# Differential attention scores: one step per unit for both softmax maps, on the lower and the upper rows of the array

## The chip, the cores and the metric

The kernel runs on one core of one Trainium2 chip. The metric is the device time of one execution in microseconds (us); lower is better. The engines are called as in the profile: PE is the matrix engine, with PEld for its weight loads, DVE the vector engine, ACT the scalar (activation) engine, POOL GpSimd, SP the queue that issues the weight DMAs.

## The reference, cut to what matters

Two layers of a mixer run over 512 latent tokens and 128 context tokens. In each layer a normalised, modulated h goes into one wide projection and then four branches. The branch that is changed is differential attention with 4 heads, each with two softmax maps over the same values:

```python
s = jnp.einsum('bqhmd,bkhmd->bhmqk', qb, k) * scale      # m = 0, 1: two maps, d = 64 each
p = jax.nn.softmax(s, axis=-1)
a = p[:, :, 0] - lam * p[:, :, 1]
return jnp.einsum('bhqk,bkhe->bqhe', a.astype(v.dtype), v)
```

A latent query sees 640 keys, 512 latent ones and 128 cached context ones. A context query sees its own 128 keys. Each map has a maximum, an exponential and a sum of its own. Everything is float32.

## The kernel before, in words

The whole program is a list of steps that `plan()` writes; every engine walks the same list in the same order and issues what it has to do in each step, so the order on each engine is fixed and an engine that waits holds all that is behind it. `SIGNALS` says how far each step moves each semaphore.

The work is tiled by 128 tokens. Tokens are tiles t = 0 to 3 (latent) and t = 4 (context). Differential attention runs over units u = 0 to 19, head f = u // 5 and tile t = u % 5. The two maps of a head lie on partitions 0 to 63 and 64 to 127 of `QT` (queries, transposed) and of `KTt` and `cK` (latent and cached keys). `differential()` writes for each unit:

- S of map 0, a place for filler work, TP of unit u-1, S of map 1, a place for filler work, PV of unit u-1. After that, for heads after the first, one part of the normalisation of the head before (NR, parts 0, 1 and 2 behind tiles 0, 1, 2) or, behind tile 4, the transposition of that head's result (YT).

The steps do the following.

- S (PE lines 1608 to 1649): 640 scores into PSUM banks 4 and 5 as one row (`scores`), as a product of 512 columns (L1647) and one of 128 (L1648); for t = 4 one of 128 (L1645). PE first waits until every exponential issued so far is done, since it overwrites the same banks. DVE takes the negated maximum (L1249), ACT takes the exponential with that bias and its sum (L952) into `Pm`. For map 1, DVE then waits for the exponentials, makes the reciprocals (L1254) and a factor (L1258) and folds map 1 into map 0 (L1261), which raises `comb`.
- TP: PE transposes the combined 128 x 640 in five pieces into banks 6 and 7 (L1666); ACT copies them to `AT` (L965).
- PV: PE multiplies by the values, five products of 128 (L1675), into a part of bank 7; DVE scales the result out (L1271) and raises `pvfree`.

The filler work is the projections of this and the next branch: `interleave()` spreads 64 parts of 12 PE instructions each (F: gate features; M: merge gates; P: output projections) over the 43 places. Their results sit in two double banks (0 and 1, 2 and 3). ACT takes a tanh of F and M (L911, L976), DVE combines F and P (L1203, L1411). They need weights: SP loads 512 KB pieces into `raw` (two buffers), ACT rounds one to `whi` (L771), POOL makes the remainder `wlo` (L701), four pieces ahead.

In layer 0 the same stage also holds 18 steps DM: each is two products with a sum on DVE (L1032) over one piece of the modulation weights, which comes through `raw` like the others. `layer_middle()` puts one behind every S step until they run out.

```python
for n, step in enumerate(rest):
    s.append(step)
    if step[0] == "S" and n < before:
        s += some(1)
```

The neighbourhood branch, later in the layer, has scores of two heads issued in turn on the two halves of the rows into banks 4 and 5 (L1638, L1641). The change leaves it as it is.

## Time and profile before

| | |
|---|---|
| median of 3 runs | 2116.16 us (2113.1 to 2120.86) |
| the profiled execution | 2114.92 us, of which 2113.1 us from the first to the last instruction |
| PE busy | 1972.8 us (93%) |
| DVE, ACT, POOL busy | 948.2, 640.1, 606.4 us |
| mean granted clock of PE | 0.976 |
| differential attention, layer 0 | about 264 to 492 us |
| differential attention, layer 1 | about 1299 to 1492 us |

How to read it: PE is busy nearly all the time and almost all of the chain that ended last runs through it. The share over the whole program says nothing on a single stage, though. In the first half of the stage in layer 0, PE is much less busy than elsewhere and DVE more.

### The profile page before, as it was taken

How to read it: one execution, taken by the hardware profiler on the slowest of the kernel's cores; microseconds unless marked ns; L12 is line 12 of the kernel's file. 1: busy time of each engine (PE TensorE's matmuls, PEld its weight loads, DVE VectorE, ACT ScalarE, POOL GpSimd, SP SyncE). 2: the span in 40 equal slices, each digit the busy share in tenths (PEclk: the TensorE clock that was granted, in tenths of full speed). 3: DMA queues.
4: the chain of work that ended last, by engine and by line, in shares of the span. 5: the costliest groups of instructions: out<-in, count | busy, mean ns of one | idle time of the engine just before them, and what ended most of it. 6: DMA issues, size and time to landing. Idle time of an engine off the chain costs nothing.

```text
span 2113.1 us, 30534 instructions
## 1 busy us (share of the span) xinstructions
PE 1972.8 (93%) x12364; PEld 1782.6 (84%) x12364; DVE 948.2 (45%) x1489; ACT 640.1 (30%) x1085; POOL 606.4 (29%) x286
## 2 busy tenths in 40 slices
PE   2798988999999999999978999999999999999998
PEld 0597777889888999899967977888898899989996
DVE  3866478454444564330242233455344555433122
ACT  3421232333343321221343222333243332213121
POOL 2632311223222233233323232222222223313331
PEclk7899999999999999999998999999999999999999
DMA  7234333112121122122322221111222112211231
GB/s 276 80 110 145 102 128 120 51 40 91 64 67 51 61 99 70 44 67 75 125 90 90 75 81 67 37 48 41 80 71 71 51 61 89 71 51 60 80 102 78
DMA packets 50956, 172.13 MB, mean 81 GB/s; under 512 B 6656, under 2 KB 7296, under 8 KB 50816
## 3 DMA queue, kind: packets, MB, share of 16 engines
q1 hardware_dynamic: 40736, 145.55, 20.6%
q10 hardware_dynamic: 10080, 24.63, 3.3%
q8 instruction: 98, 1.61, 0.3%
q14 instruction: 42, 0.34, 0.1%
HBM read 162.82 MB, written 7.34 MB: 81 GB/s over the span
## 4 chain that ended last, share of the span: by engine, by line
PE 77%; DVE 14%; issue 3%; DMA 2%; ACT 2%; POOL 1%; ACTq 0%; DVEq 0%; SPq 0%; POOLq 0%
PE ps L1573 53%; PE ps L1461 4%; PE ps L1463 3%; PE ps L1462 3%; DVE mixed L1032 3%; PE ps L1647 2%; PE ps L1666 2%; DMA raw<-in_wstream 2%; PE ps L1675 1%; PE ps L1685 1%; DVE Pm L1291 1%; DVE qr L1196 1%; DVE nmax L1249 1%; PE ps L1727 1%; DVE rt L1187 1%
## 5 line engine op out<-in xcount | busy, mean ns | idle before, releaser
L701 POOL TENSOR_TENSOR wlo<-raw,whi 128x1024 fp32r<-128x1024 f32 x224 | 560.6, 2503 | 1324.4 <-ACT whi L771 1322.4
L1573 PE MATMUL ps<-bufB,whi 128*128 128x320 f32 x2816 | 540.0, 314 | 7.0 <-DVE vn L1144 4.0
L1573 PE MATMUL ps<-bufA,whi 128*128 128x320 f32 x2816 | 540.9, 314 | 2.6 <-DVE z L1411 1.4
L1573 PEld LDWEIGHTS ps<-bufB,whi 128*128 128x128 f32 x2816 | 441.7, 189 | 16.9 <-issue 11.9
L1573 PEld LDWEIGHTS ps<-bufA,whi 128*128 128x128 f32 x2816 | 442.4, 189 | 12.7 <-issue 7.8
L1573 PE MATMUL ps<-bufB,wlo 128*128 128x320 f32 x1408 | 322.7, 310 | 0.0
L1573 PE MATMUL ps<-bufA,wlo 128*128 128x320 f32 x1408 | 322.6, 310 | 0.0
L771 ACT ACTIVATE whi<-raw 128x1024 fp32r<-128x1024 f32 x224 | 237.4, 1060 | 267.2 <-PE ps L1573 120.1
L1573 PEld LDWEIGHTS ps<-bufA,wlo 128*128 128x128 f32 x1408 | 237.3, 189 | 0.0
L1573 PEld LDWEIGHTS ps<-bufB,wlo 128*128 128x128 f32 x1408 | 237.1, 189 | 0.0
L952 ACT ACTIVATE Pm<-ps,nmax 128x640 f32<-128x640 f32 (+2 forms) x160 | 100.0, 625 | 367.2 <-DVE nmax L1249 329.4
L1411 DVE SCALAR_TENSOR_TENSOR z<-gate_m,ps 128x640 f32<-128x640 f32 x48 | 39.4, 821 | 230.0 <-PE ps L1573 229.9
L1249 DVE TENSOR_REDUCE nmax<-ps 128x1 f32<-128x640 f32 (+2 forms) x160 | 97.8, 611 | 93.4 <-PE ps L1648 65.5
L1461 PE MATMUL ps<-whi,bufA 128*128 128x512 f32 x240 | 99.4, 414 | 16.4 <-POOL bufA L736 8.4
L1032 DVE CUSTOM_DVE_ANT_0 mixed<-raw,mixed 128x1024 f32<-128x1024 f32 x64 | 94.7, 1479 | 32.5 <-DMA raw<-in_wstream 30.7
L976 ACT ACTIVATE gate_m<-ps 128x640 f32<-128x640 f32 x64 | 45.1, 705 | 192.8 <-PE ps L1573 189.7
L1461 PE MATMUL ps<-whi,bufB 128*128 128x512 f32 x240 | 95.7, 399 | 4.4 <-DVE rt L1187 3.8
L1463 PE MATMUL ps<-whi,bufA 128*128 128x512 f32 x240 | 97.3, 405 | 0.0
L1462 PE MATMUL ps<-wlo,bufA 128*128 128x512 f32 x240 | 97.0, 404 | 0.0
L1463 PE MATMUL ps<-whi,bufB 128*128 128x512 f32 x240 | 94.0, 392 | 0.0
L1462 PE MATMUL ps<-wlo,bufB 128*128 128x512 f32 x240 | 94.0, 392 | 0.0
L1647 PE MATMUL ps<-KTt,QT 64*128 64x512 f32 x128 | 72.7, 648 | 13.1 <-ACT Pm L952 11.2
(206 smaller groups left out, 1954.1 us busy)
## 6 DMA issues: line engine op xcount, KB each, us to landing
raw<-in_wstream SPq DMA_DIRECT2D x256, 512.0 KB, 3.3
stage<-in_w_mod SPq DMA_DIRECT2D x16, 512.0 KB, 15.4
out_y_sample<-X ACTq DMA_DIRECT2D x8, 512.0 KB, 2.7
Pm<-in_rpb ACTq DMA_DIRECT2D x12, 256.0 KB, 2.8
X<-in_x_sample SPq DMA_DIRECT2D x4, 512.0 KB, 12.5
xres<-in_x_sample ACTq DMA_DIRECT2D x4, 512.0 KB, 5.3
xres<-out_y_sample ACTq DMA_DIRECT2D x4, 512.0 KB, 5.5
tabs<-in_dft ACTq DMA_DIRECT2D x2, 965.5 KB, 4.6
```

Of the source, the lines that this page charges most:

```text
L701: pool.tensor_tensor(wlo[:, s % SPLITS, :], raw[:, PLAN.entry["W", s] % RAWS, :], whi[:, s % SPLITS, :].bitcast(F32), ALU.subtract).then_i ...
L771: act_e.activation(whi[:, s % SPLITS, :], raw[:, e % RAWS, :], ACT.Copy).then_inc(sems["hi"], 1)
L952: act_e.activation(dst, src, ACT.Exp, bias=nmax[:, slot:slot + 1], accum_out=esum[:, slot:slot + 1]).then_inc(sems["expd"], 1)
L976: act_e.activation(halves(gate_m[:, m % 2, :]), dsplit(b), ACT.Tanh, scale=0.5).then_inc(sems[f"free{b}"], 1)
L1032: yield dve.tensor_tensor_reduce(dots_out, src, rows[:, c, :], 0.5, 0.0, ALU.mult, ALU.add, mods[:, l, 2 * m + c:2 * m + c + 1])
L1249: dve.tensor_reduce(nmax[:, slot:slot + 1], src, AX_X, ALU.max, negate=True).then_inc(sems["nmax"], 1)
L1461: pe.matmul(out, stat_hi, mov_hi, start=first, stop=False)
L1462: pe.matmul(out, stat_hi, mov_lo, start=False, stop=False)
L1463: return pe.matmul(out, stat_lo, mov_hi, start=False, stop=last)
L1573: ins = pe.matmul(ps[:, 2 * b + n, 0:HALF], wt[:, cols], src[:, part, base + k, n * HALF:(n + 1) * HALF], start=k == 0 and wt is hi and pa ...
L1647: pe.matmul(scores[:, 0:DEC], q, KTt[row:row + 64, f, 0:DEC], start=True, stop=True)
L1666: ins = pe.transpose(dst[:, c * P:(c + 1) * P], src[:, c * P:(c + 1) * P], ident[:])
```

## The change

S becomes one step for both maps.

- PE issues the latent keys in two pieces of 256, each piece for map 0 (partitions 0 to 63, bank 4) and then map 1 (64 to 127, bank 5), and signals `sready`. Then it waits for `atready` and `pvfree`, issues the 128 context scores of both maps into the ends of banks 6 and 7 (`ctx_scores`), and signals again.
- DVE takes one maximum over the two banks (128 x 2 x 512), one over the context scores that ACT has copied to `Pm`, and the smaller of the two negated ones. Only after that ACT starts its exponentials: two of 512, and two of 128 over the copied scores, each pair with its own signal and its own sums. DVE waits for all four, adds the sums, and goes on as before.
- ACT has a new copy of the context scores (128 x 2 x 128), and the copy of the transposed weights is cut in two, since those lie in two banks now (384 and 256 columns). TP also waits for `copied`.
- In the plan, a unit is now: S, place, TP of u-1, place, PV of u-1. The number of places and the fillers in them are the same: two parts between S and TP, one between TP and PV in nearly every unit. DM now stands behind S and behind PV.

The diff, cut to its core (allocations, the list of semaphores and lines that only move are left out):

```diff
-    ("S", "diff", False, 0): {"expd": 1, "nmax": 1, "sready": 1},
-    ("S", "diff", False, 1): {"chain": 1, "comb": 1, "expd": 1, "nmax": 1, "sready": 1, "stat": 1},
+    ("S", "diff", False, 0): {"chain": 1, "comb": 1, "copied": 1, "expd": 2, "nmax": 3, "sready": 2, "stat": 2},
     ("F", "dgate"): {"dready": 1, "free": 1, "tanhd": 1},
     ("TP", "diff", False): {"atready": 1, "tpready": 1},
     ("PV", "diff", False): {"pvfree": 1, "pvready": 1},
-    ("S", "diff", True, 0): {"expd": 1, "nmax": 1, "sready": 1},
-    ("S", "diff", True, 1): {"chain": 1, "comb": 1, "expd": 1, "nmax": 1, "sready": 1, "stat": 1},
+    ("S", "diff", True, 0): {"chain": 1, "comb": 1, "expd": 1, "nmax": 1, "sready": 1, "stat": 1},
...
     for u, (f, hh, t) in enumerate(units):
-        out.append(("S", "diff", u, f, hh, t, 0))
-        out.append(None)
+        out += [("S", "diff", u, f, hh, t, 0), None]
         if u:
             out.append(("TP", "diff", u - 1, *units[u - 1]))
-        out += [("S", "diff", u, f, hh, t, 1), None]
+        out.append(None)
...
-        if step[0] == "S" and n < before:
+        if step[0] in ("S", "PV") and n < before:
...
-        scores = ps[:, 4:6, :].rearrange("p a c -> p (a c)")
-        turned = ps[:, 6:8, :].rearrange("p a c -> p (a c)")
-        out_pv = ps[:, 7, P:2 * P]
+        scores = ps[:, 4:6, :]
+        turned = ps[:, 6:8, 0:3 * P]
+        turned_at = [(6, 0), (6, P), (6, 2 * P), (7, 0), (7, P)]
+        ctx_scores = ps[:, 6:8, 3 * P:4 * P]
+        out_pv = ps[:, 7, 2 * P:3 * P]
...
-                            n = P if t == 4 else NTOK
-                            dst, src = Pm[:, slot, 0:n], scores[:, 0:n]
+                            n = P if t == 4 else DEC
+                            if u >= 2:
+
+                                act_e.wait_ge(sems["tpready"], count.step("tpready", PLAN.unit["TP", name, u - 2]))
+                            if t < 4:
+                                act_e.wait_ge(sems["sready"], count.step("sready"))
+                                act_e.activation(Pm[:, slot:slot + 2, DEC:NTOK], ctx_scores, ACT.Copy).then_inc(sems["copied"], 1)
+                                act_e.wait_ge(sems["copied"], count.own("copied"))
+                            act_e.wait_ge(sems["nmax"], count.step("nmax"))
+                            for h in range(2):
+                                ins = act_e.activation(Pm[:, slot + h, 0:n], scores[:, h, 0:n], ACT.Exp,
+                                                       bias=nmax[:, slot + h:slot + h + 1], accum_out=esum[:, slot + h:slot + h + 1])
+                            ins.then_inc(sems["expd"], 1)
+                            act_e.wait_ge(sems["expd"], count.own("expd"))
+                            if t < 4:
+                                for h in range(2):
+                                    ins = act_e.activation(Pm[:, slot + h, DEC:NTOK], Pm[:, slot + h, DEC:NTOK], ACT.Exp,
+                                                           bias=nmax[:, slot + h:slot + h + 1], accum_out=ectx[:, slot + h:slot + h + 1])
+                                ins.then_inc(sems["expd"], 1)
+                                act_e.wait_ge(sems["expd"], count.own("expd"))
+                            continue
...
-                        src = turned[:, 0:n] if name == "diff" else ps[:, 6 + u % 2, 0:n]
                         if u >= 2:
 
                             last = u - 2 if name == "diff" else u - u % 2 - 2
                             act_e.wait_ge(sems["pvready"], count.step("pvready", PLAN.unit["PV", name, last]))
                         act_e.wait_ge(sems["tpready"], count.step("tpready"))
-                        dst = AT[:, u % 2, 0:n] if name == "diff" else turned_sb[:, u % 2, 0:n]
-                        act_e.activation(dst, src, ACT.Copy).then_inc(sems["atready"], 1)
+                        if name == "na":
+                            act_e.activation(turned_sb[:, u % 2, 0:n], ps[:, 6 + u % 2, 0:n], ACT.Copy).then_inc(sems["atready"], 1)
+                        elif t == 4:
+                            act_e.activation(AT[:, u % 2, 0:P], turned[:, 0, 0:P], ACT.Copy).then_inc(sems["atready"], 1)
+                        else:
+                            act_e.activation(AT[:, u % 2, 0:3 * P], turned[:, 0, :], ACT.Copy)
+                            act_e.activation(AT[:, u % 2, 3 * P:NTOK], turned[:, 1, 0:2 * P], ACT.Copy).then_inc(sems["atready"], 1)
...
-                            slot, src = (2 * u + m) % 4, scores[:, 0:P if t == 4 else NTOK]
-                        else:
-                            slot, src = u % 4, ps[:, 4 + u % 2, 0:P if t == 4 else SPAN]
-                        dve.wait_ge(sems["sready"], count.step("sready", PLAN.unit["S", name, u | 1] if name == "na" else None))
-                        if name == "na" and t < 4:
+                            slot, r = 2 * u % 4, u % 4 * 2
+                            n = P if t == 4 else DEC
+                            pair = slice(slot, slot + 2)
+                            dve.wait_ge(sems["sready"], count.step("sready", k=1))
+                            part = nmax[:, pair] if t == 4 else nparts[:, 0, :]
+                            dve.tensor_reduce(part, scores[:, :, 0:n], AX_X, ALU.max, negate=True).then_inc(sems["nmax"], 1)
+                            dve.wait_ge(sems["nmax"], count.own("nmax"))
+                            if t < 4:
+                                dve.wait_ge(sems["copied"], count.step("copied"))
+                                dve.tensor_reduce(nparts[:, 1, :], Pm[:, pair, DEC:NTOK], AX_X, ALU.max, negate=True).then_inc(sems["nmax"], 1)
+                                dve.wait_ge(sems["nmax"], count.own("nmax"))
+                                dve.tensor_tensor(nmax[:, pair], nparts[:, 0, :], nparts[:, 1, :], ALU.min).then_inc(sems["nmax"], 1)
+                                dve.wait_ge(sems["nmax"], count.own("nmax"))
+                            dve.wait_ge(sems["expd"], count.step("expd"))
+                            if t < 4:
+                                dve.tensor_tensor(esum[:, pair], esum[:, pair], ectx[:, pair], ALU.add).then_inc(sems["stat"], 1)
+                                dve.wait_ge(sems["stat"], count.own("stat"))
+                            dve.reciprocal(rsum[:, r:r + 2], esum[:, pair]).then_inc(sems["stat"], 1)
+                            dve.wait_ge(sems["stat"], count.own("stat"))
+                            n = P if t == 4 else NTOK
+                            dve.scalar_tensor_tensor(comb_c[:, 0:1], rsum[:, r + 1:r + 2], lam[:, layer, 6:7],
+                                                     esum[:, slot:slot + 1], ALU.mult, ALU.mult).then_inc(sems["chain"], 1)
+                            dve.wait_ge(sems["chain"], count.own("chain"))
+                            dve.scalar_tensor_tensor(Pm[:, slot, 0:n], Pm[:, slot + 1, 0:n], comb_c[:, 0:1],
+                                                     Pm[:, slot, 0:n], ALU.mult, ALU.add).then_inc(sems["comb"], 1)
+                            dve.wait_ge(sems["comb"], count.own("comb"))
+                            continue
...
-                        if m == 1:
-                            n, slot, r = P if t == 4 else NTOK, 2 * u % 4, u % 4 * 2
-                            dve.wait_ge(sems["expd"], count.step("expd"))
-                            dve.reciprocal(rsum[:, r:r + 2], esum[:, slot:slot + 2]).then_inc(sems["stat"], 1)
-                            dve.wait_ge(sems["stat"], count.own("stat"))
-                            if True:
-
-                                dve.scalar_tensor_tensor(comb_c[:, 0:1], rsum[:, r + 1:r + 2], lam[:, layer, 6:7],
-                                                         esum[:, slot:slot + 1], ALU.mult, ALU.mult).then_inc(sems["chain"], 1)
-                                dve.wait_ge(sems["chain"], count.own("chain"))
-                                dve.scalar_tensor_tensor(Pm[:, slot, 0:n], Pm[:, slot + 1, 0:n], comb_c[:, 0:1],
-                                                         Pm[:, slot, 0:n], ALU.mult, ALU.add).then_inc(sems["comb"], 1)
-                                dve.wait_ge(sems["comb"], count.own("comb"))
...
-                        elif t == 4:
-                            ins = pe.matmul(scores[:, 0:P], q, KTt[row:row + 64, f, DEC:NTOK], start=True, stop=True)
-                        else:
-                            pe.matmul(scores[:, 0:DEC], q, KTt[row:row + 64, f, 0:DEC], start=True, stop=True)
-                            ins = pe.matmul(scores[:, DEC:NTOK], q, cK[row:row + 64, f, :], start=True, stop=True)
+                        maps = [slice(0, 64), slice(64, 128)]
+                        tok = slice(t * P, (t + 1) * P)
+                        if t == 4:
+                            for h, half in enumerate(maps):
+                                ins = pe.matmul(scores[:, h, 0:P], QT[half, f, tok], KTt[half, f, DEC:NTOK], start=True, stop=True)
+                            ins.then_inc(sems["sready"], 1)
+                            continue
+                        for keys in (slice(0, 256), slice(256, 512)):
+                            for h, half in enumerate(maps):
+                                ins = pe.matmul(scores[:, h, keys], QT[half, f, tok], KTt[half, f, keys], start=True, stop=True)
+                        ins.then_inc(sems["sready"], 1)
+                        pe.wait_ge(sems["atready"], count.before("atready"))
+                        pe.wait_ge(sems["pvfree"], count.before("pvfree"))
+                        for h, half in enumerate(maps):
+                            ins = pe.matmul(ctx_scores[:, h, :], QT[half, f, tok], cK[half, f, :], start=True, stop=True)
...
+                        if name == "diff":
+                            pe.wait_ge(sems["copied"], count.before("copied"))
```

How the order moves at three places. On PE, layer 0, from the transposition of unit 1 to the scores of unit 3 (L1573 and L1609 are the filler products, L1666 and L1713 TP, L1675 and L1722 PV), before:

```order
L1666 MATMUL ps<-ident,Pm 128x128 x5
L1647 MATMUL ps<-KTt,QT 128x512
L1648 MATMUL ps<-cK,QT 128x128
L1573 MATMUL ps<-bufA,whi 128x320 x4
L1573 MATMUL ps<-bufA,wlo 128x320 x2
L1573 MATMUL ps<-bufA,whi 128x320 x4
L1573 MATMUL ps<-bufA,wlo 128x320 x2
L1675 MATMUL ps<-V,AT 128x128 x4
L1675 MATMUL ps<-cV,AT 128x128
L1647 MATMUL ps<-KTt,QT 128x512
L1648 MATMUL ps<-cK,QT 128x128
```

and of the change:

```order
L1713 MATMUL ps<-ident,Pm 128x128 x5
L1609 MATMUL ps<-bufA,whi 128x320 x4
L1609 MATMUL ps<-bufA,wlo 128x320 x2
L1609 MATMUL ps<-bufA,whi 128x320 x4
L1609 MATMUL ps<-bufA,wlo 128x320 x2
L1722 MATMUL ps<-V,AT 128x128 x4
L1722 MATMUL ps<-cV,AT 128x128
L1687 MATMUL ps<-KTt,QT 128x256 x4
L1692 MATMUL ps<-cK,QT 128x128 x2
```

The scores that stood between TP and PV are gone from there; only one part of filler is left between them.

On ACT, unit 8 (tanh of a merge gate L976 or L1000, rounding of a weight piece L771 or L772, copies of TP L965 or L988 and L989), before:

```order
L952 ACTIVATE Pm,esum<-ps,nmax 128x640 x2
L976 ACTIVATE gate_m<-ps 128x640
L771 ACTIVATE whi<-raw 128x1024
L965 ACTIVATE AT<-ps 128x640
L952 ACTIVATE Pm,esum<-ps,nmax 128x640
L952 ACTIVATE Pm,esum<-ps,nmax 128x128
```

and of the change:

```order
L948 ACTIVATE Pm<-ps 128x2x128
L952 ACTIVATE Pm,esum<-ps,nmax 128x512 x2
L958 ACTIVATE Pm,ectx<-Pm,nmax 128x128 x2
L1000 ACTIVATE gate_m<-ps 128x640
L772 ACTIVATE whi<-raw 128x1024
L988 ACTIVATE AT<-ps 128x384
L989 ACTIVATE AT<-ps 128x256
L952 ACTIVATE Pm,esum<-ps,nmax 128x128 x2
```

All exponentials of a unit now stand ahead of the copy that PV of the unit before waits for.

On DVE, unit 2 in layer 0 (L1271 and L1307 scale a result of PV out, L1032 and L1056 are the products of DM), before:

```order
L1271 TENSOR_SCALAR yb<-ps,rsum 128x128
L1249 TENSOR_REDUCE nmax<-ps 128x1
L1032 ISA mixed,mods<-raw,mixed 128x1024
L1032 ISA mods 128x1
L1032 ISA mixed,mods<-raw,mixed 128x1024
L1032 ISA mods 128x1
L1249 TENSOR_REDUCE nmax<-ps 128x1
L1254 RECIPROCAL rsum<-esum 128x2
L1258 SCALAR_TENSOR_TENSOR comb_c<-rsum,lam,esum 128x1
L1261 SCALAR_TENSOR_TENSOR Pm<-Pm,comb_c 128x640
```

and of the change:

```order
L1307 TENSOR_SCALAR yb<-ps,rsum 128x128
L1056 ISA mixed,mods<-raw,mixed 128x1024
L1056 ISA mods 128x1
L1056 ISA mixed,mods<-raw,mixed 128x1024
L1056 ISA mods 128x1
L1269 TENSOR_REDUCE nparts<-ps 128x2
L1273 TENSOR_REDUCE nparts<-Pm 128x2
L1275 TENSOR_TENSOR nmax<-nparts 128x2
L1279 TENSOR_TENSOR esum<-esum,ectx 128x2
L1281 RECIPROCAL rsum<-esum 128x2
L1284 SCALAR_TENSOR_TENSOR comb_c<-rsum,lam,esum 128x1
L1287 SCALAR_TENSOR_TENSOR Pm<-Pm,comb_c 128x640
```

The DM that stood inside the unit is ahead of it, and nothing is left between the maxima and the sums that DVE could do while ACT works.

## Rows read from the trace of the kernel before

**Rows 1.** Stretches: us, busy of PE, PEld, DVE, ACT, POOL, PEclk, DMA share, GB/s.
```profile
264.00:372.00 108.00, 94.27 (x522) 79.00 (x521) 87.58 (x146) 32.45 (x60) 19.69 (x8) 0.94 0.38 127
372.00:492.00 120.00, 116.20 (x719) 101.64 (x719) 61.79 (x120) 41.94 (x78) 26.51 (x13) 1.00 0.15 49
1299.00:1492.00 193.00, 188.34 (x1128) 161.26 (x1129) 92.55 (x179) 70.24 (x129) 39.58 (x18) 0.99 0.13 43
```
**Rows 2.** Waits of PE, 264 to 372 us: us in total, times, longest.
```profile
PE ps L1647 <- ACT Pm L952: 8.3, 8, 2.9
```
**Rows 3.** Waits of DVE, same stretch.
```profile
DVE mixed L1032 <- DMA raw<-in_wstream: 3.6, 5, 2.6
```
**Rows 4.** Waits of PE in layer 1's stage, 1299 to 1492 us.
```profile
PE ps L1647 <- ACT Pm L952: 2.3, 2, 1.7
```
**Rows 5.** Timeline of layer 1, PE rows: start us, us, operation, count.
```profile
1325.72 1.12 PE L1647 MATMUL ps<-KTt,QT 64*128 64x512 f32 x2
...
1326.99 0.85 PE L1573 MATMUL ps<-bufB,whi 128*128 128x320 f32 x4
...
1330.62 0.71 PE L1666 MATMUL ps<-ident,Pm 128*128 128x128 f32 x5
...
1331.26 1.12 PE L1647 MATMUL ps<-KTt,QT 64*128 64x512 f32 x2
...
1334.39 1.05 PE L1675 MATMUL ps<-V,AT 128*128 128x128 f32 x8
...
1335.60 0.48 PE L1645 MATMUL ps<-KTt,QT 64*128 64x128 f32 x2
```
**Rows 6.** Timeline of PE, a pair of neighbourhood scores.
```profile
514.78 0.70 PE L1638 MATMUL ps<-KTt,QT 64*128 64x256 f32 x4
515.31 0.39 PE L1641 MATMUL ps<-cK,QT 64*128 64x128 f32 x4
515.63 0.44 PE L1666 MATMUL ps<-ident,Pm 128*128 128x128 f32 x2
```
**Rows 7.** Lines, shapes kept apart: count, busy us, mean ns, idle before.
```profile
L771 ACT ACTIVATE whi<-raw 128x1024 fp32r<-128x1024 f32 x224 | 237.4, 1060 | 267.2 <-PE ps L1573 120.1 <-DMA raw<-in_wstream 71.2 <-PE ps L1463 38.6
...
L1249 DVE TENSOR_REDUCE nmax<-ps 128x1 f32<-128x640 f32 x64 | 52.8, 825 | 66.8 <-PE ps L1648 65.5
...
L952 ACT ACTIVATE Pm<-ps,nmax 128x640 f32<-128x640 f32 x64 | 50.9, 796 | 193.8 <-DVE nmax L1249 174.7 <-PE ps L1666 11.1 <-DMA out_new_diff_v<-V 7.8
...
L976 ACT ACTIVATE gate_m<-ps 128x640 f32<-128x640 f32 x64 | 45.1, 705 | 192.8 <-PE ps L1573 189.7 <-issue 2.1
...
L965 ACT ACTIVATE AT<-ps 128x384 f32<-128x384 f32 x64 | 31.5, 492 | 11.7 <-PE ps L1666 9.7
...
L952 ACT ACTIVATE Pm<-ps,nmax 128x128 f32<-128x128 f32 x32 | 11.8, 368 | 59.9 <-DVE nmax L1249 41.2 <-PE ps L1666 17.7
...
L1249 DVE TENSOR_REDUCE nmax<-ps 128x1 f32<-128x128 f32 x32 | 9.3, 292 | 24.3 <-PE ps L1645 17.8 <-PE ps L1641 5.5
...
L1254 DVE RECIPROCAL rsum<-esum 128x2 f32<-128x2 f32 x40 | 6.6, 166 | 41.7 <-ACT Pm L952 41.7
```
**Rows 8.** Timeline of DVE in layer 0's stage.
```profile
333.60 0.49 DVE L1308 TENSOR_SCALAR z<-yb 128x640 f32<-128x640 f32 x1
...
335.51 0.82 DVE L1249 TENSOR_REDUCE nmax<-ps 128x1 f32<-128x640 f32 x1
...
346.22 0.82 DVE L1315 TENSOR_REDUCE ss<-z 128x5 f32<-128x640 f32 x1
...
347.69 0.82 DVE L1249 TENSOR_REDUCE nmax<-ps 128x1 f32<-128x640 f32 x1
348.55 1.22 DVE L1032 CUSTOM_DVE_ANT_0 mixed<-raw,mixed 128x1024 f32<-128x1024 f32 x1
...
351.09 0.82 DVE L1249 TENSOR_REDUCE nmax<-ps 128x1 f32<-128x640 f32 x1
```
**Rows 9.** Stretch of 4 us in layer 0's stage, columns as in rows 1.
```profile
336.00:340.00 4.00, 2.61 (x5) 1.34 (x6) 2.81 (x6) 1.59 (x3) 0.00 (x0) 0.50 0.30 124
```

16 lines of the change are left out of this document (10 added, 6 removed).

## The prediction

> **What bounds the kernel now.** The change touches only differential attention, so I read that stage, once in each layer. The view by stretches [rows 1] splits it in three. In the first half in layer 0, where the DM steps are, PE is busy 94 of 108 us at a clock of 0.94, and DVE 88 of 108. In the second half PE has 116 of 120 us, in layer 1 188 of 193, both at a clock near 1, with DVE half idle. So the first 108 us belong to DVE and the rest to PE. The waits say the same: PE waits for exponentials at the scores 8 times, 8.3 us in all, in the first part [rows 2], and only 2 times, 2.3 us, in layer 1 [rows 4].
>
> **PE's saving.** A map's 640 scores take 1326.99 - 1325.72 = 1.27 us [rows 5], two maps 2.54. The changed form exists already in the neighbourhood branch: 256 keys for each of two heads, in turn on both halves of the rows, take 515.31 - 514.78 = 0.53 us, and 128 keys 0.32 [rows 6]. Two pieces of 256 and one of 128 are 1.38 us. A latent unit saves 1.16 us. A context unit has 128 keys only; I take 0.4, within the bounds of nothing and 1.16. Outside the DM part there are 8 latent and 3 context units in layer 0 (10.5 us) and 16 and 4 in layer 1 (20.2 us).
>
> The rows of the pair give 2.54 / 1.38, a factor of 1.84, with the weight loads and handoffs in it. The Trainium skill, TensorEngine Tiling (Array Packing), Theoretical Speedup, says up to 2x for a contraction of 64 or less. By that the scores would take 1.27 us and the saving outside the DM part would be some 2.6 us larger, an estimate that stays inside my range.
>
> **The new chain from scores to exponentials.** Before, DVE and ACT dealt with one map while PE did fillers, and between TP and PV there were scores and a part of filler. Now the whole chain of two maps comes first, and ACT's copy that PV needs is queued behind it. From the start of S on PE, with DVE free:
> - The latent scores end at 1.06; with the pipeline's tail and a handoff DVE starts at about 1.35.
> - The maximum over 1024 columns: 640 take 0.825 and 128 take 0.292 [rows 7], slope 1.04 ns per column, so 1.23 us. Ends: 0.83 and 1.65 (two of 640).
> - The maximum over 2 x 128 copied columns: 0.42 by that slope; ends 0.29 and 0.83. The smaller of the two: 0.17, as the reciprocal of two columns [rows 7]. With gaps, done at 3.25.
> - Two exponentials of 512: 640 take 0.796, 128 take 0.368 [rows 7], so 0.69, and with the read of the sum 0.8 each; two of 128, 0.46 each. The last ends at 5.95.
> - The copies of the previous unit: 384 columns 0.49 [rows 7], 256 by the slope 0.39. `AT` is ready at about 6.9.
>
> PE reaches PV at 1.38 + 3.6 (two parts of filler, from 1326.99 to 1330.62) + 0.64 (TP, to 1331.26) + 1.8 = 7.4 us [rows 5]. The slack is 0.5 us, and whatever ACT or DVE has to do besides comes off it. A tanh is 0.7 and a rounding of weights 1.06 [rows 7]; both stand between the exponentials and the copy wherever the two parts of filler end a group or begin one. Normalisation stands ahead of DVE's maximum: part 0 takes 335.51 - 333.60 = 1.9 us, part 1 takes 347.69 - 346.22 = 1.5 [rows 8], and behind the drain of PV (0.5 us into the unit) they delay the maximum by 1.1 and 0.6; for part 2 I take 0.95. YT puts a DVE operation of 0.82, an ACT one of 0.7 and again 0.82 there, a delay of about 1.5. Going down the plan, PE's new waits at PV are 0.2, 0, 0.6, 0.2, 0.6, 1.2, 2.3 us for the latent units 1, 2, 3, 5, 6, 7, 8, together 5.1, and 1.0, 1.7, 1.9, 0.5, 2.1, 2.4, 0.1, 0.5 for 10 to 13 and 15 to 18, together 10.2. The context units have short exponentials and wait for nothing.
>
> Layer 1: -20.2 + 15.3, and the 2.3 of today's waits at the scores [rows 4] go: **-7.2 us**. Layer 0 from unit 9 on: -10.5 + 10.2: **-0.3 us**. What hides the exponentials is PE's filler; without the half of it that moved from behind TP, this is what is left.
>
> **The DM part.** DVE walks its list nearly without a pause here. Per latent unit it does 1.23 + 0.42 + 0.17 us of maxima instead of 2 x 0.825, and one more addition of 0.17 with its gap. While ACT works it now has nothing to do: today it waits 41.7 / 40 = 1.04 us for one exponential [rows 7]; four need about 2.7. That is 2.1 us more per unit, 17 us over the 8 latent units. The DMs themselves only change places (3.4 us between two maxima with one in between, of which 2.54 are the DM [rows 8]), but one now falls behind unit 9's scores, where PE can cover it: -2.5. Of the 3.6 us of DVE's waits for the weight stream [rows 3] a slower DVE should meet most landed, and some of its waits for scores go: -4. PE runs further ahead of DVE and carries this lead of some 2 us into unit 9, but gives it back at PV and YT there. **+10 us**; the ends are 5 and 17. PE's saving counts nothing here.
>
> **Sum.** -7.2 - 0.3 + 10 = +2.5 us. POOL, SP and all other stages are unchanged and stay hidden. The profiled execution took 2114.92 us, 1.2 below the median of the runs; from it I get 2117, which is also the median within the spread of 7.8 us between runs. About 0.5%, 10.6 us, is what a measurement of this kernel can tell from no change.
>
> One number decides more than others: the length of the chain. Each 0.1 us on it costs 0.8 in the DM part and about 2 at the 20 waits elsewhere. Its parts with their ends put it between 5.2 and 6.8 instead of 5.95.
>
> **Rivals.**
> 1. *The chain is short and the saving stands* (15%). With 5.2 us, most of the waits at PV vanish: layer 1 gains 8 more, layer 0's second part 5, the DM part 6: 2098. For it speaks that DVE and ACT may read the copied scores and two banks at once cheaper than the slope of single forms says. Against it: the rows of 128 and 640 of both engines lie on one slope.
> 2. *PE falls to its lower clock in the DM part* (17%), the case on the slow side. In the 4 us after PE had been idle for most of a stretch, the granted clock was 0.50 [rows 9], the 1.2 GHz level. In that part PE would have 8.6 us of work in a unit of 12.2, with waits in each. At full clock it ends PV some 2 us before DVE asks for it. If more than half of a unit's PE work runs at the lower level, that margin is gone, and PE adds 1 to 2 us to each of 8 units: 2129. Against it: today's idle time there mostly leaves the clock alone, 0.94 on average [rows 1].
> 3. *The chain is long* (6%): 6.8 us, +24: 2141. The evacuation becomes the bound everywhere. The Trainium skill, TensorEngine Tiling (Array Packing), PSUM Bottleneck, warns of this: tiling speeds up TensorE but not the evacuation of PSUM. In layer 1 the busy times speak against it as a bound by work: DVE has 93 us and ACT 70 of 193 [rows 1]; only their latency could do it.
> 4. *The two maps don't overlap* (3%). Then PE saves nothing and even so pays for the new order: the 10 us of the DM part, and of the waits at PV those that are longer than 1.16 us, some 8 less today's 2.3: about +16, 2131. The neighbourhood rows [rows 6], with the same shapes, types and halves, speak against it.
>
> **How the numbers follow.** The forecast, no change that can be measured, has 59%: 2117, with a range of its own of 2107 to 2126. Rival 1 is faster by over 0.5%, 15%, to which 2% of the forecast's tail is added. Rivals 2 to 4 are slower, 26%, less 2% of rival 2 that stays within 0.5%. The range from 2099 to 2133 takes in rival 1 nearly to its centre, all of the slower clock, and leaves out the long chain.
>
> **What would show it.** Right: the pairs of 256 at 0.53 us; new idle time of PE at the PV products, released by ACT's copy, of 10 to 20 us a layer; the reciprocals' wait on DVE at about 2.7 us each; the DM part longer by about 10 us, the layer 1 stage shorter by about 7. Wrong: no waits at PV (rival 1), a DM part with a mean clock under 0.85 that is longer by 20 (rival 2), or waits at PV in nearly every unit, with the layer 1 stage no shorter (rival 3).

## The result, and the profile after

The changed kernel takes 2145.93 us (median of 4 runs, 2143.87 to 2148.69) against 2117.03 of the kernel before (4 runs): a ratio of 1.014, 95% interval 1.012 to 1.016. That is 1.4% slower, above the range of the prediction. The profiled execution took 2148.69 us with a span of 2146.9; the span before was 2113.1.

I cut both traces at the same four events: the first scores of differential attention and the first latent scores of the neighbourhood branch, in both layers.

| piece of the program | before | after | difference | forecast |
|---|---|---|---|---|
| layer 0's stage | 249.88 | 284.55 | +34.7 | +9.7 |
| of it, from unit 0's to unit 9's maximum (the DM part) | 103.83 | 133.80 | +30.0 | +10 |
| layer 1's stage | 233.63 | 230.19 | -3.4 | -7.2 |
| all the rest | | | +2.5 | 0 |

The stretches that answer to [rows 1], with its columns: the DM part, the second part of layer 0's stage, and layer 1's.

```profile
265.00:402.00 137.00, 96.51 (x565) 87.92 (x565) 93.64 (x157) 40.72 (x109) 19.83 (x8) 0.81 0.28 92
402.00:527.00 125.00, 109.31 (x736) 102.31 (x737) 66.96 (x138) 49.06 (x124) 26.81 (x13) 0.93 0.17 55
1334.00:1523.00 189.00, 170.03 (x1192) 158.69 (x1193) 96.63 (x206) 85.79 (x225) 40.65 (x18) 0.97 0.14 44
```

In the DM part no engine is near full any more: PE 97 of 137 us, DVE 94. The granted clock is 0.81. In layer 1 PE does less work (170 us of 189, where it was 188 of 193 before) and the stretch is hardly shorter.

DVE's other long waits before the change, beside the one in [rows 3] and in the same stretch:

```profile
DVE rsum L1254 <- ACT Pm L952: 10.3, 9, 1.4
DVE nmax L1249 <- PE ps L1648: 2.3, 2, 1.6
```

Whom DVE waits for in the DM part after it (264 to 400 us), answering to [rows 3], and PE in the same stretch, answering to [rows 2]:

```profile
DVE esum L1279 <- ACT Pm L958: 20.4, 8, 2.6
DVE mixed L1056 <- DMA raw<-in_wstream: 13.6, 5, 3.5
DVE yb L1307 <- PE ps L1722: 2.2, 1, 2.2
DVE nparts L1269 <- PE ps L1687: 1.4, 1, 1.4
```

```profile
PE ps L1722 <- ACT AT L989: 26.3, 7, 7.7
PE ps L1692 <- DVE yb L1307: 11.0, 4, 4.9
```

DVE waits 2.6 us for the exponentials in each of 8 units, 10 us more than before for the stream of weights, and only 3.6 us for PE. PE in turn waits for ACT's copy at PV (L1722) and for DVE's drain of PV (L1307, the scaling of its result out of PSUM) at the context scores (L1692). The copy is queued behind the exponentials, which wait for DVE's maxima, and the drain stands in DVE's own list, so both are late because DVE is.

The lines that answer to [rows 7], in the same stretch:

```profile
L1687 PE MATMUL ps<-KTt,QT 64*128 64x256 f32 x64 | 11.9, 503 | 1.5 <-issue 0.9 <-ACT Pm L958 0.6
L952 ACT ACTIVATE Pm<-ps,nmax 128x512 f32<-128x512 f32 x16 | 10.8, 683 | 39.2 <-DVE nmax L1275 39.2
L1269 DVE TENSOR_REDUCE nparts<-ps 128x2 f32<-128x1024 f32 x8 | 9.8, 1224 | 1.6 <-PE ps L1687 1.4
L1273 DVE TENSOR_REDUCE nparts<-Pm 128x2 f32<-128x256 f32 x8 | 3.4, 420 | 0.3
L1275 DVE TENSOR_TENSOR nmax<-nparts 128x2 f32<-128x2 f32 x8 | 1.3, 161 | 0.3
L1056 DVE CUSTOM_DVE_ANT_0 mixed<-raw,mixed 128x1024 f32<-128x1024 f32 x34 | 53.9, 1584 | 14.6 <-DMA raw<-in_wstream 13.6
```

The parts of the chain are what the slopes said: 1.22, 0.42 and 0.16 us for the maxima, 0.68 for an exponential of 512. What the prediction had not listed is the last row: a DM product (one of the two products of a DM step) takes 1.58 us on average. In the stretch before, 36 of them took 1.34:

```profile
L1032 DVE CUSTOM_DVE_ANT_0 mixed<-raw,mixed 128x1024 f32<-128x1024 f32 x36 | 48.3, 1340 | 4.7 <-DMA raw<-in_wstream 3.6
```

**Two things happen to the DM steps.** Here they are in one unit, DVE first, then POOL, ACT and SP's queue:

```profile
311.01 0.16 DVE L1279 TENSOR_TENSOR esum<-esum,ectx 128x2 f32<-128x2 f32 x1 [2.56 <-ACT Pm L958]
...
311.67 0.89 DVE L1287 SCALAR_TENSOR_TENSOR Pm<-Pm,comb_c 128x640 f32<-128x640 f32 x1
312.59 3.25 DVE L1056 CUSTOM_DVE_ANT_0 mixed<-raw,mixed 128x1024 f32<-128x1024 f32 x1
...
315.88 1.23 DVE L1056 CUSTOM_DVE_ANT_0 mixed<-raw,mixed 128x1024 f32<-128x1024 f32 x1
...
317.15 0.35 DVE L1307 TENSOR_SCALAR yb<-ps,rsum 128x128 f32<-128x128 f32 x1
320.54 1.23 DVE L1056 CUSTOM_DVE_ANT_0 mixed<-raw,mixed 128x1024 f32<-128x1024 f32 x1 [3.03 <-DMA raw<-in_wstream]
```

```profile
312.14 2.61 POOL L702 TENSOR_TENSOR wlo<-raw,whi 128x1024 fp32r<-128x1024 f32 x1 [25.45 <-ACT whi L772]
```

```profile
310.94 1.06 ACT L772 ACTIVATE whi<-raw 128x1024 fp32r<-128x1024 f32 x1
```

```profile
317.15 0.80 SPq L675 DMA_DIRECT2D raw<-in_wstream  x2
```

First: the product that starts at 312.59 runs beside POOL's subtraction (312.14 to 314.75) and ends at 315.84, 1.09 us after it, as if it had begun only then. Its neighbour takes 1.23. There are 2 such products of over 2 us in the DM part before and 6 after. In 3 of the 6 (at 272.64, 312.59 and 371.14) the order itself brings the two together: a rounding of weights on ACT that has waited behind the exponentials ends about 1 us after them, and wakes POOL just when DVE has combined the maps and turns to the DM. In the other 3 the second product of a DM step meets POOL, as in the 2 before the change.

Second: a raw buffer comes free when its DM is done (317.11), SP issues the next load at 317.15, and the next DM on DVE can start at 320.54. Before the change at least a maximum (0.8 us) lay between two DM steps besides the drains; now it is the drain alone, here 0.35 us, and 3 us of the transfer have nothing to cover them.

By DVE's own account the part is longer by 11.1 us of waits for exponentials, 10.0 for the stream, 6.8 of busy time and 1.3 of waits for PE: 29.2 of the 30.0.

**In layer 1** PE's waits answer to [rows 4]:

```profile
PE ps L1722 <- ACT AT L989: 13.4, 9, 3.4
PE ps L1722 <- ACT AT L986: 4.0, 3, 1.7
```

In the last unit 1.8 us were there before. And this is PE after a short and a long one of these waits, in the timeline:

```profile
1412.71 1.16 PE L1722 MATMUL ps<-V,AT 128*128 128x128 f32 x8 [1.99 <-ACT AT L989]
...
1488.05 2.08 PE L1722 MATMUL ps<-V,AT 128*128 128x128 f32 x8 [3.40 <-ACT AT L989]
...
1490.49 2.08 PE L1687 MATMUL ps<-KTt,QT 64*128 64x256 f32 x8
```

(Each float32 product leaves two records, so x8 are four products.) After 3.40 us of waiting the same eight records take 2.08 us instead of 1.16, and so do those of the scores that follow (2.08, in the next unit, at 1500.33, 1.13). The granted clock from 1488.0 to 1493.5 us is 0.50, the lower level, 1.2 GHz. A wait of 2.05 us (before 1391.29) was followed by such a stretch too, one of 1.99 us (before 1412.71) was not.

### The profile page after: what moved, and what is told of

Its sections match the earlier page's. It is cut to its first block, busy times and chain, and to the rows that moved or that the text cites. A ratio compares the mean times of both kernels' runs of the same rounds, so it can differ in the third digit from the quotient of the medians.

```text
span 2146.9 us, 31093 instructions
## 1 busy us (share of the span) xinstructions
PE 1953.9 (91%) x12492; PEld 1795.1 (84%) x12492; DVE 959.2 (45%) x1545; ACT 670.9 (31%) x1277; POOL 605.5 (28%) x286
## 3 DMA queue, kind: packets, MB, share of 16 engines
q1 hardware_dynamic: 40736, 145.55, 20.2%
## 4 chain that ended last, share of the span: by engine, by line
PE 70%; DVE 17%; ACT 6%; issue 4%; DMA 2%; POOL 1%; ACTq 0%; DVEq 0%; SPq 0%; POOLq 0%
PE ps L1609 49%; DVE mixed L1056 4%; PE ps L1497 3%; PE ps L1499 3%; PE ps L1498 3%; ACT Pm L952 2%; PE ps L1722 2%; DMA raw<-in_wstream 2%; PE ps L1713 2%; DVE nparts L1269 2%; PE ps L1732 1%; DVE Pm L1327 1%; ACT whi L772 1%; DVE qr L1220 1%; ACT Pm L958 1%
## 5 line engine op out<-in xcount | busy, mean ns | idle before, releaser
L1609 PE MATMUL ps<-bufA,whi 128*128 128x320 f32 x2816 | 545.1, 316 | 3.6 <-DVE z L1447 1.4
L1609 PE MATMUL ps<-bufB,whi 128*128 128x320 f32 x2816 | 541.7, 315 | 6.8 <-DVE vn L1168 3.9
L1609 PEld LDWEIGHTS ps<-bufA,whi 128*128 128x128 f32 x2816 | 447.1, 191 | 11.8 <-issue 9.9
L1609 PEld LDWEIGHTS ps<-bufB,whi 128*128 128x128 f32 x2816 | 444.0, 190 | 14.6 <-issue 12.3
L1609 PE MATMUL ps<-bufA,wlo 128*128 128x320 f32 x1408 | 325.0, 312 | 0.0
L1609 PE MATMUL ps<-bufB,wlo 128*128 128x320 f32 x1408 | 322.9, 311 | 0.0
L772 ACT ACTIVATE whi<-raw 128x1024 fp32r<-128x1024 f32 x224 | 237.4, 1060 | 265.0 <-PE ps L1609 125.2
L1609 PEld LDWEIGHTS ps<-bufA,wlo 128*128 128x128 f32 x1408 | 239.5, 191 | 0.0
L1609 PEld LDWEIGHTS ps<-bufB,wlo 128*128 128x128 f32 x1408 | 237.5, 189 | 0.0
L1056 DVE CUSTOM_DVE_ANT_0 mixed<-raw,mixed 128x1024 f32<-128x1024 f32 x64 | 103.2, 1612 | 39.7 <-DMA raw<-in_wstream 37.9
L1000 ACT ACTIVATE gate_m<-ps 128x640 f32<-128x640 f32 x64 | 45.0, 704 | 196.5 <-PE ps L1609 194.1
L1722 PE MATMUL ps<-V,AT 128*128 128x128 f32 x272 | 46.2, 317 | 57.8 <-ACT AT L989 49.9
L1722 PEld LDWEIGHTS ps<-V,AT 128*128 128x128 f32 x272 | 39.4, 219 | 65.1 <-ACT AT L989 55.7
L972 ACT ACTIVATE Pm<-ps,nmax 128x384 f32<-128x384 f32 (+1 forms) x80 | 43.1, 538 | 151.1 <-DVE nmax L1298 133.2
## 6 DMA issues: line engine op xcount, KB each, us to landing
stage<-in_w_mod SPq DMA_DIRECT2D x16, 512.0 KB, 15.4
```

The source lines that it names most:

```text
L772: act_e.activation(whi[:, s % SPLITS, :], raw[:, e % RAWS, :], ACT.Copy).then_inc(sems["hi"], 1)
L972: act_e.activation(dst, src, ACT.Exp, bias=nmax[:, slot:slot + 1], accum_out=esum[:, slot:slot + 1]).then_inc(sems["expd"], 1)
L1000: act_e.activation(halves(gate_m[:, m % 2, :]), dsplit(b), ACT.Tanh, scale=0.5).then_inc(sems[f"free{b}"], 1)
L1056: yield dve.tensor_tensor_reduce(dots_out, src, rows[:, c, :], 0.5, 0.0, ALU.mult, ALU.add, mods[:, l, 2 * m + c:2 * m + c + 1])
L1609: ins = pe.matmul(ps[:, 2 * b + n, 0:HALF], wt[:, cols], src[:, part, base + k, n * HALF:(n + 1) * HALF], start=k == 0 and wt is hi and pa ...
L1722: ins = pe.matmul(out_pv, AT[:, u % 2, c * P:(c + 1) * P], v, start=c == 0, stop=c == len(tiles) - 1)
```

## The experiments

I set out with two theories. **Theory 1**: DVE's list sets the DM part, and what the change adds to it (bare waits for exponentials, waits for the stream, held-up products) costs the 30 us. **Theory 2**, rival 2 of the prediction: PE at its lower clock sets it. The clock of 0.81 is just what I had named as rival 2's mark. Times stand against runs of the kernel before on the same chip (2115 to 2118 us). "Stage" is cut as in the table above.

### The stage without DM steps, in both orders

```
-        s += [("F", "sgg", f)] + some(1) + [("F", "sgu", f), ("SG", f)] + some(1)
+        s += [("F", "sgg", f)] + some(4) + [("F", "sgu", f), ("SG", f)] + some(4)
```

> The kernel before, with 24 of the 32 DM steps of layer 0 put into the gating branch ahead of differential attention (three more behind each of its eight places), so that none is left inside the differential stage. It is the base for the next run. Both theories: the first part of the stage in layer 0 is then as dense as layer 1's (PE over 95% busy, no waits of DVE for the weight stream), and what it gains, some 10 us, is given back in part where the DMs now stand. 2105 to 2125.

> The changed kernel with the same move of the DM steps. Theory 1 (the loss is DVE's in the DM part: 30 of the 34 us by the profile lie there, as longer waits for exponentials, waits for the weight stream and slowed DM products): without DMs in the stage it stands within 6 us of the run of the kernel before with the same move. Theory 2 (the loss is PE's: waits at the PV products and the lower clock behind them): it stays slower by 15 us or more, since these are there with or without DMs.

Measured: the old order 2155.76 us (4 runs), the new one 2147.18 (4 runs); layer 0's stage 237.86 and 230.75 us, layer 1's 235.08 and 230.00. Without DMs among the units the change gains 8.6 us, 7.1 of them in the stage where it had lost 34.7. The loss belongs to the DM steps, and theory 2 is out as it stood: it wanted 15 us or more of loss here. My number for the old order (2105 to 2125) was missed by over 30 us: with most DMs at the front, the stage starts 57 us later than before (322.17 against 264.90), and ahead of it PE waits 27.7 us for DVE at three places.

### The DM into the wait for the exponentials

The combining of the maps becomes a step C of its own behind the DM; PE's order stays that of the change.

```
-        out += [("S", "diff", u, f, hh, t, 0), None]
+        out += [("S", "diff", u, f, hh, t, 0), ("C", "diff", u, f, hh, t), None]
```

> The changed kernel with the sums, reciprocals and combination of DVE put into a step of their own behind the DM, so that DVE does a DM (2.54 us) while ACT takes the four exponentials (2.56 us). Theory 1: the waits for exponentials in the DM part nearly go (20 us to under 5), and the time falls by 15 to 20 us, to about 2128. Theory 2: DVE was not the bound, the time falls by under 6 us. If the waits for the weight stream (13.6 us) take up the slack, they grow by as much and the time falls by under 8.

Measured: 2111.42 us (10 runs), ratio to before 0.998 (0.996 to 0.999); stage 248.39. One move on DVE takes back 34.5 us, about twice what I had expected of theory 1, since I had counted only the exponentials and the stream and the held-up products went too. DVE's waits from 265 to 400 us:

```profile
DVE yb L1315 <- PE ps L1730: 12.6, 7, 2.2
DVE esum L1297 <- ACT Pm L962: 7.7, 3, 2.6
DVE mixed L1060 <- DMA raw<-in_wstream: 2.9, 4, 1.3
```

The exponentials' wait stays where no DM fills it; the stream's falls from 13.6 to 2.9, because there is again DVE work between two DMs; products of over 2 us fall from 6 to 1 in the DM part (from 8 to 2 among the 42 that start after 200 us). DVE now waits for PE, and the clock from 265 to 370 us is 0.93:

```profile
265.00:370.00 105.00, 84.69 (x569) 77.78 (x569) 86.93 (x164) 42.36 (x111) 18.59 (x8) 0.93 0.37 125
```

PE's instructions and their order are those of the change. So the low clock came with PE's idle time and went with it; it was not what made the part late.

### The order of the score products

```
-                        for keys in (slice(0, 256), slice(256, 512)):
-                            for h, half in enumerate(maps):
+                        for h, half in enumerate(maps):
+                            for keys in (slice(0, 256), slice(256, 512)):
```

> The changed kernel with the four products of the latent keys in the order map 0, map 0, map 1, map 1 instead of in turn; everything else the same. If the two halves of the rows overlap only when issued in turn, the four take about 1.7 instead of 0.94 us, and in layer 1, where the slack before the PV products is 0.5 us or less, the stage grows by some 8 to 16 us less the waits at PV that this hides. If the rows overlap anyway, or the time of the scores is set by something else, 0.94 us stays and the total too.

Measured: 2141.85 us (2 runs), 4 below the change. The four products (eight records) as two of map 0, then two of map 1:

```profile
1330.47 1.14 PE L1687 MATMUL ps<-KTt,QT 64*128 64x256 f32 x8 [0.90 <-issue]
```

The change has 1.13 in the same place. The pairing does not need the products issued in turn. That this run was a little faster comes from layer 1 (225.87, clock 0.99, no wait over 2.1 us), and I don't claim it as an effect of the order: the ratios to before, 1.012 (1.009 to 1.016) and 1.014 (1.012 to 1.016), overlap.

### The pieces alone

The kernel before, its 512 columns as two products of 256, still one map at a time:

```
-                            pe.matmul(scores[:, 0:DEC], q, KTt[row:row + 64, f, 0:DEC], start=True, stop=True)
+                            for keys in (slice(0, 256), slice(256, 512)):
+                                pe.matmul(scores[:, keys], q, KTt[row:row + 64, f, keys], start=True, stop=True)
```

> The kernel before with one edit: each map's product of 512 columns is issued as two of 256, all else in the old order, a map at a time. If the saving comes from the lower and upper rows working at once, a map's products cost what they cost before (0.96 us, or two records of some 0.48), and the time is the same within 0.5% (2110 to 2122). If a part of the saving is in the size of the pieces, a map's 512 columns fall towards 0.5 us, each of the two stages gets 8 to 15 us shorter, and the whole comes to 2085 to 2105, which would beat the change by an edit of one line.

Measured: 2114.53 us (10 runs), ratio 0.998 (0.997 to 0.999); stages 252.1 and 233.7, against 249.9 and 233.6. One map's four records:

```profile
1301.44 1.10 PE L1648 MATMUL ps<-KTt,QT 64*128 64x256 f32 x4 [0.90 <-issue]
```

Four records for one map take 1.10 us, eight for two maps 1.13. The saving is the two halves of the array at work together, and nothing of it the size of the pieces.

### The transposes first

With C as above, the transposes of unit u-1 go ahead of the scores of u, so that ACT's copy for PV is queued ahead of the exponentials (PE waits for `copied` ahead of PV besides).

```
+        if u:
+            out.append(("TP", "diff", u - 1, *units[u - 1]))
         out += [("S", "diff", u, f, hh, t, 0), ("C", "diff", u, f, hh, t), None]
-        if u:
-            out.append(("TP", "diff", u - 1, *units[u - 1]))
-        out.append(None)
         if u:
             out.append(("PV", "diff", u - 1, *units[u - 1]))
...
+        out.append(None)
```

> The changed kernel with the combining of the two maps as a step of its own behind the DM (as in e3), and with the transposes of the previous unit moved ahead of the scores of the current one, so that ACT's copy of them is queued ahead of the exponentials. If the waits at PV come from that copy standing behind the exponentials: the waits of PE for it (13.4 us in layer 1 and about as much in layer 0 after unit 9) fall to under 4 a layer, the layer 1 stage from 230.2 to 215 to 222 us, layer 0's from e3's 248.4 to 235 to 243, the whole to 2085 to 2100, under both kernels. If the evacuation is a bound by its work (the long chain) the idle time only changes place: waits at the transposes or the scores of the same size, layer 1's stage at 228 or more, the whole at 2108 or more.

Measured: 2102.43 us (4 runs), ratio 0.993 (0.991 to 0.995); stages 244.3 and 226.7. It beats both kernels, by less than I expected, and both expectations are half right: the wait for ACT's copy is gone (0.4 us left in layer 1), but neither stage nor the whole came into the range I had for that case, and PE waits elsewhere, as the rival had it, though for less (14.1 us at the transposes of layer 1, where it was 17.4 at PV). In layer 1:

```profile
PE ps L1721 <- DVE yb L1315: 11.5, 8, 3.3
PE ps L1721 <- DVE Pm L1305: 2.6, 1, 2.6
```

The transposes (L1721) write the banks where PV's result lies, and its drain on DVE is queued behind the combining, which waits for the exponentials. The obvious next step is to drain first:

```
-        out += [("S", "diff", u, f, hh, t, 0), ("C", "diff", u, f, hh, t), None]
+        out += [("S", "diff", u, f, hh, t, 0), None]
         if u:
             out.append(("PV", "diff", u - 1, *units[u - 1]))
+        out.append(("C", "diff", u, f, hh, t))
...
-        if step[0] in ("S", "PV") and n < before:
+        if step[0] in ("S", "C") and n < before:
```

> As e5, with the combining step behind PV of the unit before instead of ahead of it (order of a unit: transposes, scores, filler, PV, combining, filler). In e5 PE waits 11.5 us in layer 1 at the transposes, released by DVE's drain of PV (longest 3.3): that drain is queued behind the combining, which waits for the exponentials. If this queue on DVE is what is left of the chain: those waits fall under 4 us, layer 1's stage from 226.7 to 215 to 221, the whole to 2080 to 2096. If the exponentials themselves end too late for the filler there is: the wait moves to DVE's combining as releaser, with 8 us or more, and the stage stays at 223 or more.

Measured: 2138.46 us (4 runs), 36 slower than the step before; stages 255.8 and 251.9. The rival held, and worse than it said. In layer 1:

```profile
PE ps L1722 <- DVE Pm L1306: 31.3, 17, 4.3
```

The combining now stands behind the drain of PV on DVE, and PV lies behind a filler on PE (DVE waits 48.2 us for it at the drain in this stage), and what follows the combining (the transposes) gets too little cover: 17 times PE waits. A small part is again POOL: two combinings of this stage start beside its subtraction (1397.7 and 1466.3 us) and take 3.04 and 2.88 us instead of 0.89; in the change none of 32 does.

### The weight stream

A third raw buffer has room only if one of the 5 buffers for split weights (`whi`, `wlo`) goes, so that the base has 4.

```
-RAWS = 2
-SPLITS = 5
+RAWS = 3
+SPLITS = 4
...
-            for e in range(RAWS, len(PLAN.stream)):
+            for e in range(2, len(PLAN.stream)):
```

> The changed kernel with 4 instead of 5 buffers for the split weights. It is the base for e8, which has no room otherwise. Theory 1 (waits for the weight stream and slowed DM products make up the DM part): a bit slower than the change, 2146 to 2165, with DVE's waits for the stream between 264 and 400 us at about 13 us or more. Rival (the DM part is long by the exponentials alone): no dependence on these buffers, 2146 +- 5.

> As e7, with a third buffer for the raw weight stream. Theory 1: DVE's waits for the stream fall from some 13 us to under 5 and layer 0's stage gets 5 to 12 us shorter than in e7; the slowed DM products stay. Rival: the waits move to other places of DVE and the stage stays within 3 us of e7's.

> The kernel before with 4 split and 3 raw buffers: the control for e8, whose 27 us against e7 may be due to the change's DM part or be had with the old order too. Theory 1 (the change itself made the stream a bound): before waits only 3.6 us for the stream, so at most 4 to 8 us of layer 0's middle are to be had, and elsewhere whatever e8 got outside that part (about 16 of its 27: it reached the stage 7 earlier, and 10 between the layers), so 2095 to 2108. Rival (a third buffer helps every order alike): 2090 or less.

| kernel | 2 raw buffers | 3 raw buffers | its stage in layer 0 |
|---|---|---|---|
| order of the change, 4 split | 2143.77 (2 runs) | 2116.75 (8 runs) | 284.1 to 272.8 |
| order before, 5 and 4 split | 2117.32 (8 runs) | 2095.47 (4 runs) | 249.9 to 247.9 |
| DM in the wait | 2111.42 (10 runs) | 2095.17 (5 runs) | 248.4 to 248.1 |
| transposes first | 2102.43 (4 runs) | 2091.68 (4 runs) | 244.3 to 244.6 |

With the third buffer DVE has no wait for the stream left in the changed kernel's DM part:

```profile
DVE esum L1279 <- ACT Pm L958: 20.4, 8, 2.6
DVE rsum L1281 <- ACT Pm L952: 2.0, 2, 1.0
DVE nparts L1269 <- PE ps L1687: 1.4, 1, 1.4
```

That is worth 11.3 us of the stage in the new order and 2.0 in the old: some 9 us of the change's loss are the stream. The held-up products stayed, as expected (8 in the DM part, 6 without the third buffer). The third buffer also gains 5 to 13 us between the two stages and 3 to 10 ahead of the first, with either order; that was never the change's doing. The fifth split buffer makes no difference to the order of the change (2143.77 with 4, 2145.93 with 5; theory 1 had expected 2146 or more with 4); for the old order it was not tried alone.

> The kernel of e3 (the DM in the wait for the exponentials, order of PE as in the change) with 4 split and 3 raw buffers. Against e8 (272.8 in layer 0's stage) it tells what the place of the DM is worth when the stream is no bound. Theory (in the change DVE's waits for exponentials of 2.6 us a unit and the DM products held up by POOL are added to DVE's list): the stage 244 to 250, some 25 us shorter than e8's, waits for exponentials between 264 and 400 under 8 us (23.0 in e8), at most 3 DM products over 2 us in the whole of the first layer's DMs (9 in e8); the whole 2086 to 2096. Rival (it was the stream, and the place of the DM matters only through it): within 5 us of e8's stage, 2112 or more.

Measured: 2095.17 us (5 runs), stage 248.1, 25 shorter than with the DM behind the combining (272.8). The theory held: those 25 us are the exponentials and the held-up products (9 of over 2 us after 200 us in the kernel of the table's first row, 2 here), not the stream. With the 9 of the stream they make up 34 of the 34.7 us, and the stage is as long as that of the old order with the same buffers (247.9). And since the third buffer gives this kernel's stage nothing (248.4 without it), the stream was a long wait only while DVE's list was badly spread.

> As e9, with 4 split and 3 raw buffers (as e8). Adds to e9 what the weight stream is still worth: DVE's waits for it between 264 and 400 us (7.0 us in e5) go to about 0, the whole 3 to 10 us under e9; if the stream is hidden there anyway, the same as e9 within 2.

Measured: 2124.90 us (5 runs), stages 259.2 and 249.2: neither of the two cases; it is 13.6 us under its base with 2 raw buffers, but the stage in question got 3.4 longer, and the gain lies outside. It tells of the buffers what the table tells.

> The kernel of e5 (combining as its own step behind the DM, transposes of the previous unit ahead of the scores) with 4 split and 3 raw buffers. If the weight stream and the order of DVE's steps were all that the change lacked: DVE's waits for the stream between 264 and 400 us at about 0 (7.0 in e5), layer 0's stage 236 to 243 (e5 244.3, e11 247.9), the whole 2074 to 2088, at least 8 us under e11's 2095.5. If the change is worth nothing by itself once both kernels have three raw buffers: within 5 us of 2095.

Measured: 2091.68 us (4 runs), ratio 0.987 (0.985 to 0.988), the fastest of the kernels here that leave nothing out. Its stages are 244.6 and 226.9 us, against 247.9 and 235.2 of the old order with the same buffers: 11.6 us less. In the median only 3.8 of them are left (2091.68 and 2095.47, ratios to before 0.985 to 0.988 and 0.988 to 0.992, on different chips); between the stages and ahead of them this kernel was 7 us longer. So my case for it (2074 to 2088, 8 us or more under the old order) was missed, and by the whole time it is the other case that came out, within 5 us of 2095, though the stages say otherwise. Why isn't settled: the steps outside are the same, and the piece between the stages took 772 to 779 us in the five kernels with three raw buffers.

### POOL's subtraction cut short

This kernel leaves the low parts of 960 of the 1024 columns of every weight piece at zero; it is there for the times alone.

```
-                pool.tensor_tensor(wlo[:, s % SPLITS, :], raw[:, PLAN.entry["W", s] % RAWS, :],
-                                   whi[:, s % SPLITS, :].bitcast(F32), ALU.subtract).then_inc(sems["lo"], 1)
+                pool.tensor_tensor(wlo[:, s % SPLITS, 0:64], raw[:, PLAN.entry["W", s] % RAWS, 0:64],
+                                   whi[:, s % SPLITS, 0:64].bitcast(F32), ALU.subtract).then_inc(sems["lo"], 1)
```

> The changed kernel with POOL's subtraction for the low part of the weights cut from 1024 columns to 64 (the low parts of the other columns are left at zero). If a DM product that starts beside that subtraction is held up by it: no DM product in the middle of layer 0 over 2 us (8 before), DVE busy there 8 us less, and raw buffers free 2.5 us earlier, so stage 0 from 284.6 to 262 to 276. If the slow products have another cause (landing DMA, the shape), they stay at 6 or more, and only the earlier release counts: 276 to 283.

Measured: no DM product over 2 us among all 64 (13 in the change, 6 of them in the DM part). The two rows, of DVE and of POOL, in its DM part:

```profile
L1057 DVE CUSTOM_DVE_ANT_0 mixed<-raw,mixed 128x1024 f32<-128x1024 f32 x35 | 42.9, 1225 | 15.1 <-DMA raw<-in_wstream 14.1
...
L703 POOL TENSOR_TENSOR wlo<-raw,whi 128x64 fp32r<-128x64 f32 x7 | 4.5, 649 | 93.2 <-ACT whi L773 93.2
```

Every product now takes 1.225 us, and the waits for the stream are as before (14.1): the hold-up is POOL's, and it is apart from the stream. Stage 268.8 us, 15.8 shorter, in the range. Not all of it is the products: 6 times 2.02 us is 12, and in layer 1, where there are no DM steps, the stage is shorter too (223.9). The whole takes 2070.08 us (2 runs), most of that gained outside the two stages; it is no measure of the change. PE does not gain it by having the low parts earlier: in the change it waits 0.6 us for them. What falls are its waits for DVE, between the stages from 30.5 to 15.4 us. The traces suggest why: other DVE instructions start beside the subtraction too and are held up like the DM products (last section). The old order with the short subtraction was not run.

## Why the prediction was wrong

The forecast was no measurable change, 2117 us within 2099 to 2133. The time is 2145.93.

- **PE's saving.** 1.16 us for a latent unit and 0.4 for a context unit were right to a little low: S takes 1.28 us, from 265.37 to the filler at 266.65, where I had 1.38, and in a context unit both maps take 0.42 us (1366.57 to 1366.99), as one map did (307.52 to 307.94). In layer 1 PE's busy time fell by 226.81 - 208.74 = 18.1 us, where I had 20.2. The rest fits the clock, below: in the run with the other order of products, at 0.99, it fell to 205.20, by 21.6. Rival 4, no overlap, is out.
- **The chain.** Right. From the start of S to the last exponential 5.6 us, where I had 5.95 (265.37 to 270.97), and every part within 0.15. The new waits at PV: 15.3 us forecast for layer 1, 15.6 measured (13.4 + 4.0 - 1.8). That they agree so well is in part luck: 2.2 of the 15.6 are at the PV of context units (4.0 - 1.8), which were to wait for nothing. In layer 0 behind unit 9, 10.2 forecast, 11.8 measured. Rivals 1 and 3 are out.
- **Layer 1, -7.2.** It came to -3.4. The sum treated PE's waits as idle time and nothing more. Behind the longest ones PE works at half the clock for a while: the stretch's clock fell from 0.99 to 0.97, idle time rose by 14.6 (13.0 forecast), and busy time fell 2.1 less than forecast. The second part of layer 0 looks the same: +4.7 instead of -0.3, at a clock of 0.93 where it had been 1.00.
- **The DM part, +10.** This is the step that failed: +30.0. Its first term was 3 us too high: 17 for the exponentials and maxima, less 2.5 for the DM that moved behind unit 9, stands against 11.1 of waits for exponentials and 2.6 of added work (9.8 + 3.4 + 1.3 + 1.3 us for 8 units, where 16 maxima of 0.825 stood), less the same 2.5. The second term was wrong in sign, and this is the larger miss: "Of the 3.6 us of DVE's waits for the weight stream a slower DVE should meet most landed ... -4". The waits for the stream rose by 10.0, from 3.6 to 13.6, and those for PE by 1.3, 15 us from the -4. I had looked at how fast DVE eats the stream on average, and not at the gap from a DM that frees a buffer to the next that needs it, which is what 2 buffers and a transfer of 3.3 us look at. "The DMs themselves only change places" was the third error: in their new place they meet POOL, some 8 us more for 4 more products held up. Two of these were in the trace of before, at 3.3 instead of 1.23 us, and I had not looked at the single products.
- **Rival 2.** Its mark came true (clock 0.81, 30 us longer), and its cause did not: DVE waited for PE 3.6 us, and with the DM moved the part was short again. A low clock does not tell a late PE from one that is kept waiting; whether DVE waits for PE does. Its time, 2129, lay nearer than mine for a wrong reason.
- **The slow side** had 24%, and none of its cases has this mechanism in it; rival 3's 2141 lay nearest, with a chain of 6.8 us that was 5.6. The range stopped at 2133 because all its bounds came from rows of single instructions; none came from an order in which two waits meet.

## What to carry to other kernels

When a step that shares a small ring of buffers with a DMA is moved, look at the time on its engine from the step that frees a buffer to the next step that needs one, not at the mean rate; two such steps with next to nothing between them cost nearly a whole transfer (here 3.0 of 3.3 us). If a chain gets longer latency for less work, put the work of the engine that waits inside the wait (here the DM between maxima and combining, worth 34.5 us) before counting any saving. And count a long wait of PE (here 3.4 us) at more than its length: what follows it ran at half the clock.
